# The first 55 microseconds of a two-part transformer kernel: x as the second load, vector copies on ScalarE, wide column products and more warming matmuls

## What is computed

```
c_act = silu(c)
mod = c_act @ w_ada[l] + b_ada[l]
sh_m, sc_m, gt_m, sh_f, sc_f, gt_f = split(mod, 6)
h = rms_norm(x, g_mix[l]) * (1 + sc_m) + sh_m
proj = h @ w_in[l]
qa, ka, va, qb, kb, vb, gate_logits = split(proj, ...)
```

## Time and profile before

| | us |
|---|---|
| runs of the kernel before | 1434.23, 1434.84, 1433.21 (median 1434.23) |
| the profiled execution's own time | 1432.99 |
| its span, first to last instruction | 1431.1 |
| TensorE busy (share of the span) | 1390.8 (97%) |
| VectorE busy | 924.7 (65%) |
| ScalarE busy | 757.9 (53%) |
| DMA, mean over the span | 192 GB/s |

### The profile page before, as it was taken

How to read it: one execution, slowest core, us unless ns; L and a number is a source line. 1 busy time by engine, 2 the same in 40 slices (tenths; PEclk the granted TensorE clock), 3 DMA queues, 4 the chain that set the end, 5 groups by cost and what they waited for, 6 DMA issues and landing times.

```text
span 1431.1 us, 19203 instructions
## 1 busy us (share of the span) xinstructions
PE 1390.8 (97%) x7039; PEld 1156.4 (81%) x7039; DVE 924.7 (65%) x1401; ACT 757.9 (53%) x1249; POOL 80.4 (6%) x133
## 2 busy tenths in 40 slices
PE   4999999999999999999899999999999999999998
PEld 4878877899988888887778888888888877788886
DVE  5677786798777554478986555476545556675453
ACT  4457746655456444366576444455444567574442
POOL 3011100000000000021300000000000100000000
PEclk9999999999999999999999999999999999999999
DMA  9897655477745755544355665547555463565540
GB/s 352 289 306 244 203 180 177 156 257 235 242 142 186 231 186 189 168 133 148 118 176 184 220 199 177 176 138 259 178 192 191 125 207 118 191 231 181 187 166 30
DMA packets 177596, 274.36 MB, mean 192 GB/s; under 512 B 6465, under 2 KB 120897, under 8 KB 177505
## 3 DMA queue, kind: packets, MB, share of 16 engines
q1 hardware_dynamic: 170800, 250.87, 52.9%
q0 software_dynamic: 5552, 20.20, 4.6%
q10 hardware_dynamic: 1153, 2.07, 0.5%
HBM read 272.05 MB, written 1.06 MB: 191 GB/s over the span
## 4 chain that ended last, share of the span: by engine, by line
PE 76%; DVE 5%; issue 1%; ACT 1%; DMA 0%; POOL 0%; DVEq 0%; POOLq 0%; SPq 0%; ACTq 0%
PE psum L2541 22%; PE psum L2543 22%; PE psum L2542 22%; PE psum L2581 2%; PE psum L2584 2%; PE psum L2583 2%; PE psum L2786 1%; DVE w_lo L2136 1%; PE psum L2638 1%; PE psum L2710 1%; PE psum L2739 0%; DVE PR L2476 0%; DVE attn L2313 0%; PE psum L2653 0%; DVE work L2290 0%
## 5 line engine op out<-in xcount | busy, mean ns | idle before, releaser
L2136 DVE TENSOR_TENSOR w_lo<-raw,w_hi 128x1024 fp32r<-128x1024 f32 (+1 forms) x312 | 371.8, 1234 | 114.4 <-ACT w_hi L1925 113.5
L1925 ACT ACTIVATE w_hi<-raw 128x1024 fp32r<-128x1024 f32 (+1 forms) x312 | 310.7, 1050 | 101.2 <-PE psum L2543 64.4
L2541 PE MATMUL psum<-w_hi,hT_hi 128*128 128x512 f32 x888 | 356.1, 401 | 6.9 <-DVE hT_lo L2236 3.7
L2543 PE MATMUL psum<-w_hi,hT_lo 128*128 128x512 f32 x888 | 347.2, 391 | 0.0
L2542 PE MATMUL psum<-w_lo,hT_hi 128*128 128x512 f32 x888 | 346.9, 391 | 0.0
L2541 PEld LDWEIGHTS psum<-w_hi,hT_hi 128*128 128x128 f32 x888 | 167.4, 189 | 46.2 <-issue 10.5
L2543 PEld LDWEIGHTS psum<-w_hi,hT_lo 128*128 128x128 f32 x888 | 167.2, 188 | 36.1
L2542 PEld LDWEIGHTS psum<-w_lo,hT_hi 128*128 128x128 f32 x888 | 167.6, 189 | 32.5 <-issue 0.5
L2136 DVE TENSOR_TENSOR lo_qk<-raw,hi_qk 128x1024 fp32r<-128x1024 f32 (+1 forms) x72 | 84.1, 1207 | 31.1 <-ACT hi_qk L1925 31.0
L2541 PE MATMUL psum<-w_hi,hc_hi 128*128 128x512 f32 x256 | 100.3, 392 | 0.6 <-DVE hc_lo L2461 0.6
L2543 PE MATMUL psum<-w_hi,hc_lo 128*128 128x512 f32 x256 | 99.8, 390 | 0.0
(11 more groups left out here) (236 smaller groups left out, 2334.8 us busy)
## 6 DMA issues: line engine op xcount, KB each, us to landing
raw<-in_ffn_wg_dram SPq DMA_DIRECT2D x88, 512.0 KB, 3.9
raw<-in_ffn_wu_dram SPq DMA_DIRECT2D x88, 512.0 KB, 5.0
raw<-in_ffn_wd_dram SPq DMA_DIRECT2D x44, 1024.0 KB, 4.9
raw<-in_w_up_dram SPq DMA_DIRECT2D x44, 512.0 KB, 4.9
raw<-in_w_in_dram SPq DMA_DIRECT2D x19, 1024.0 KB, 7.5
ada_raw<-in_w_ada_dram POOLq DMA_DIRECT2D x24, 512.0 KB, 5.3
raw<-in_even_w_in_dram SPq DMA_DIRECT2D x12, 1024.0 KB, 5.1
raw<-in_odd_w_in_dram SPq DMA_DIRECT2D x12, 1024.0 KB, 5.6
```

The costliest lines, as they stand in the source:

```text
L1925: nc.scalar.activation(hi_of(s)[:, cs], raw_of(s)[:, cs], ACT.Copy).then_inc(ready, 1)
L2136: nc.vector.tensor_tensor(lo_of(u)[:, cs], raw_of(u)[:, cs], hi_of(u)[:, cs].bitcast(F32), ALU.subtract)\
L2541: nc.tensor.matmul(o, a_hi, b_hi, start=start, stop=False)
L2543: return nc.tensor.matmul(o, a_lo, b_hi, start=False, stop=stop)
```

## The change

- x is loaded by SP, behind the first unit of `w_ada`, and no longer by GpSimd's queue.
- The four copies of the vectors are made by ScalarE, behind the squares; VectorE only waits for them in front of the statistic, which has moved up between the sums of the first two `w_ada` units.
- The column products have 128 equal moving columns (`c_act` broadcast, a square of ones) in place of one. Both kinds now add up in the same place, so that VectorE needs one addition for a block in place of two; it reads every 128th column.
- `warm` waits for nothing: eight matmuls directly behind the turn of `c`, ten behind the vectors' turns, six behind the column products of block 2.
- The modulated reads of a bank are split by k-tile: two steps of one k-tile each, so `hT_lo` is made in two instructions of 128 x 256.
- The last unit of each four early ones is loaded in two halves (`early_second`).
- The plan's order: the column sum of block 0 and its bias addition come before the last sums of block 2. The split of unit 1 comes behind the first modulated reads, that of unit 2 behind the second. In the second round the column sum of block 1 comes before all sums of block 3, and va's k-tiles are spread between.

```diff
@@ build_plan @@
     ada(0, 0)
+    vector_uses = [pl.use(b) for b in (4, 5, 6, 7)]
+    pl.add("warm", bank=7, times=8)
+    st = tile_stat()
+    squared = x_squares(st, (0, 1), [("x_loaded", 16)] * TT)
+    pl.add("vectors", uses=vector_uses)
+    var(st, (0, 1), squared, False, EPS)
     shared = shared_ada(0, 0, 3)
-    vector_uses = [pl.use(b) for b in (4, 5, 6, 7)]
-    pl.add("vectors", uses=vector_uses)
-    st = x_stats([("x_loaded", 16)] * TT)
-    pl.add("warm", use=vector_uses[3], times=8)
+    pl.add("normalise", st=st, half=0)
+    pl.add("warm", bank=1, times=10)
+    turned_rows = [turn_early(G, ("scr_ready", scr_version()), ("mod", 1), ("mod", 0), 0, 2),
+                   turn_early(G, None, ("mod", 1), ("mod", 0), 2, 3)]
     ada(2, 0)
-    pl.add("normalise", st=st, half=0)
-    rest = turn_early(G, ("scr_ready", scr_version()), ("mod", 1), ("mod", 0), 0, (2, 3))
+    adasum(0, shared=shared)
     shared2 = shared_ada(2, 1, 3)
...
     pl.split_to(0)
-    adasum(0, shared=shared)
+    adasum(2, shared=shared2)
+    pl.add("warm", bank=0, times=6)
+    pl.add("modfinal", vec=1, gain=0, half=0)
+    turned_rows[0]()
     pl.split_to(1)
-    adasum(2, shared=shared2)
-    pl.add("modfinal", vec=1, gain=0, half=0)
-    rest[0]()
+    turned_rows[1]()
     pl.split_to(2)
-    rest[1]()
...
     pl.split_to(3)
+    product_step("proj", va[1][0], ks=(0,), inc=None)
+    adasum(1, shared=shared)
     ada(3, 0)
-    product_step("proj", va[1][0], ks=(0,), inc=None)
+    product_step("proj", va[1][0], ks=(1,), inc=None)
+    turned_rows = [turn_early(G, ("scr_ready", v), ("mod", 1), ("mod", 0), 4, 2)]
     shared3 = shared_ada(3, 3, 3)
-    adasum(1, shared=shared)
+    product_step("proj", va[1][0], ks=(2,), inc=None)
     adasum(3, shared=shared3)
-    rest = turn_early(G, ("scr_ready", v), ("mod", 1), ("mod", 0), 4, (2, 3))
-    product_step("proj", va[1][0], ks=(1, 2, 3))
+    product_step("proj", va[1][0], ks=(3,))
+    turned_rows.append(turn_early(G, None, ("mod", 1), ("mod", 0), 6, 3))
     pl.add("modfinal", vec=1, gain=0, half=1)
...
@@ column products @@
-                                nc.tensor.matmul(psum[:, use.bank, 4 + j:5 + j],
+                                nc.tensor.matmul(psum[:, use.bank, j * P:(j + 1) * P],
                                                  w[:, k * BANK + j * P:k * BANK + (j + 1) * P],
-                                                 c_act[:, 4 + k:5 + k], start=k == a["own"][0], stop=k == 3)
+                                                 c_act[:, 4 + k:5 + k].to_broadcast([P, P]),
+                                                 start=j == 0 and k == a["own"][0], stop=False, skip_group_check=True)
...
-                            ins = nc.tensor.matmul(psum[:, use.bank, j:j + 1], acc[:, j * P:(j + 1) * P],
-                                                   ones[:, 0:1], start=True, stop=True)
+                            ins = nc.tensor.matmul(psum[:, use.bank, j * P:(j + 1) * P], acc[:, j * P:(j + 1) * P],
+                                                   ones[:, 0:P], start=a["unit"] is None and j == 0, stop=True,
+                                                   skip_group_check=True)
```

82 lines of the change are left out of this document (46 added, 36 removed).

## The result

The change takes 1437.46 us (median of ten runs, 1436.97 to 1439.80), the kernel before 1434.78 in the ten runs beside it (1433.21 to 1436.41). The ratio is 1.0021, with a 95% interval of 1.0013 to 1.0029: **+2.7 us**. The interval leaves out 1, so the change is slower, if by only about what a measurement here can tell. The forecast was 1436.0 in a range of 1431.4 to 1439.0, most likely "no change that can be told"; the measured time lies between it and the slower rival's 1437.9. The profiled execution took 1437.91, span 1436.1. That is 4.9 over the profiled execution of before, so the two profiles differ by 2.2 us more than the medians.

A forecast was written before the change was run, and what follows sets the result against it. TensorE, busy 97%, was taken as the bound, with VectorE leading after T. T = 25.5 plus 29.3 gave U = 54.8 against 53.05, +1.75 us: 1436.0 against the median 1434.23, range 1431.4 to 1439.0.

The forecast's parts named there:

- slower rival: Ahead of U: TensorE's 3.1 us without work drops the clock, +1.7 us, to 1437.9; chance 20%.
- T: Start of ACT's first modulated turn: forecast 25.5 against 26.12 before; 23.4 with the upper clock level, 26.0 with the lower.
- The statistic: Step behind x's squares and the vector copies, ahead of the normalised rows: forecast at 13.6, 2.7 us sooner.
- the wait for the first column product: VectorE waiting for TensorE before its column add, ahead of T: 0.1 to 2.6 us, taken as 2.1.
- the warm-up holds: At the start: warming matmuls run up to the turns, clock up, T 23.4, U 52.7, time 1433.9; chance 27%.
- the second set: ACT's modulated turns started by the second modulation vector: forecast at T + 25.1, before at T + 21.7.
- The sums of block 1: VectorE's next sums after the low halves of unit 2: forecast at T + 8.25, before at T + 6.3.
- the stall: VectorE standing before the last sums of the second round, behind the column add: a new 2.15 us.
- U: Start of the fifth weight unit's first product on TensorE: forecast T + 29.3 = 54.8 against 53.05, +1.75 us.
- the last wait for TensorE's columns: TensorE's four last column products before the second vector's add and hand-over: 1.0 us.
- The row: Trace evidence for column products: eight one-column passes take 1.03 us, held by weight loads, as 128 columns do.
- What follows moves by what U moves: After U the instruction list is the same, so the time moves by U's shift, forecast +1.75 us.

The follow-up runs named there:

- second profile: The change, unaltered, profiled once more in one execution beside one of the kernel before: 1440.59 us, the kernel before 1436.59.
- filled gap: The change with twelve more warming matmuls behind va's last k-tile, ahead of the last four turns: 1434.75 us, ratio 1.0002.
- early high half: The change with the high half of unit 1 made on ACT before the first modulated turns: 1436.23 us, ratio 1.0014.
- all together: The change with the second round's sums in a row, later first addition, earlier high halves and the fifth unit's low half split: 1430.14 us, ratio 0.9973.
- reordered variant: The change with its second round (column sums of blocks 1 and 3, va's k-tiles) in the order of before: 1435.34 us, ratio 1.0003.
- wide columns: The kernel before with only the column products of 128 equal columns and the single bias addition: 1432.85 us, ratio 0.9987.
- no warming: The change without its three groups of warming matmuls (24 in all): 1438.06 us, ratio 1.0028.
- late addition: The change with the first vector's column add behind the following unit's four sums and six warming matmuls in another bank: 1437.38 us, ratio 1.0020.
- narrow columns: The change with the single-column products and the two column adds of the kernel before: 1439.64 us, ratio 1.0035.

## Why the prediction was right, and what was off

The time lies in the range, and the path was the right one: what VectorE's list gives away behind T eats the early start. But the forecast's own narrower range, +0.9 to +2.5, was missed by 0.2, the moments on the path came out right in part through misses of opposite sign, and the clock, which the forecast held at 1.00, fell.

**The start.** The statistic was forecast for 13.6 and came at 13.58, and by luck: x landed at 10.43 for 9.9, so the squares ended at 12.83 for 12.3, and the four copies behind them, put at 1.2 us, took 0.61 (12.74 to 13.35). A third miss was hidden by the squares. The vectors' rows were to land at 8 and landed at 11.17, for 11.02 before; in the other profiles with x on SP's queue they landed between 10.31 and 11.14. A queue with a megabyte less beside them helped by 0.7 us at most, not by three. By the rule of the Trainium skill, "DMA: Bandwidth & Descriptors", section Queues, rings and completion order, that each DMA engine takes the queues in turn, I had looked for an earlier landing; this trace does not show it. The copies I had bounded by ones of 8 and 256 columns and taken a middle value, but copies overlap: the second starts at 12.88, when the first, of 0.24 us from 12.74, is still running. The Trainium skill, "ScalarE: Activation LUTs", section What ACT_TABLE_LOAD costs, gives an ACTIVATE with immediate operands 186 ns and 0.833 ns a column, with an overlap of 93 ns between neighbours; by it the four would take an estimated 0.74, nearer than my figure.

**T.** Forecast 25.5, measured 24.30 and 23.81. The term that was off is the wait for the first column product: 2.1 us forecast, 1.16 and 0.66 measured. It was priced with the lower clock through the turns and most of the column products. The rival "the warm-up holds" had the mechanism for this part: with the vectors' rows late, the warming matmuls ran until 16.7, and the clock was up at 17.7, or 15.0 in the second profile. Its T of 23.4 lies 0.4 to 0.9 below, since VectorE waits a little even then. Its end, 1433.9, did not come about, for what happened behind T.

**From T to the second set.** The sums of block 1 were forecast at T + 8.25 and came at T + 8.06; the stall 2.15, measured 2.44; the second set at T + 25.1, measured T + 25.7; U at T + 29.3, measured T + 30.0 in both profiles. The forecast's own terms for the second set add up to T + 24.95. Most of the rest is the last wait for TensorE's columns, put at 1.0 and measured at 1.73 (49.53 above). This part of the prediction stands, and the runs show its causes: the high half of unit 1 behind T costs 1.0 us, the order of the second round 3.1 us in the second set (T + 22.6 for T + 25.7). U came out at +1.26 (+0.78 in the second profile) for the forecast's +1.75, because the T that was 1.2 too late was partly made up by 0.7 too little behind it.

**The clock ahead of U.** The forecast held it at 1.00; the rival with 20% let it fall and priced it at 1.7 us. It fell in both profiles, for 1.7 and 2.7 us, and in three of the four variants that left the gap, which makes five of six. So the profiled time is the forecast's path, shorter by 0.5, with this rival's price on top. For the median the argument is the filled gap, which takes 2.7 us off. The chance was too small: I had counted against it that single columns had preceded both earlier falls. It fell here with 128 columns too, so they are not needed for it, but not always, as the variant with the early high half shows (3.48 us, no fall). The gap's length alone does not settle it: a gap of 3.13 us at 79, in the variant with all together, left the clock at 1.00, and one of 1.88 in the reordered variant did in one profile and not in the other. The gap with matmuls in it kept the clock twice of two.

**Wide columns.** The row had them cost nothing, against the rule of the Trainium skill, "TensorE: Matmul & The Clock Gate", section Back-to-back issue gap. Row and runs agree (1.03 and 1.05 us), the rule's 2 us do not show. What I missed is their gain: at U I allowed 1.7 us of cleaner products and said that none of it would reach it. Alone, in the kernel before, they brought U forward by 1.24, since there TensorE's own queue, with the second set's turns and the products behind them, sets U. In the changed kernel VectorE does, as I had said.

**Behind U.** "What follows moves by what U moves" was too strong. The wait for the next modulation rows added 0.6 in the first profile, and the load near 270 added 1.1. ScalarE's wait for that load is 3.45 to 3.98 us in six profiles (before, wide columns, filled gap twice, no warming, all together) and 4.48 to 4.91 in seven (change twice, order twice, early high half, late addition, narrow columns). In the three programs profiled twice both executions agree, so it goes with the program; its cause is open, and no variant was made for it. The 1.9 between 85 and 150 in the second profile of the change is open too.

## What to carry over

A start that is 2 us earlier is worth nothing if the leader behind it is another engine whose list also grew: follow the moment to where the bounding engine runs without a gap again. Adding an in-order wait on VectorE for TensorE's result costs all that stands behind it, so put the work that waits for nothing ahead of the addition. And price every gap of some microseconds on TensorE twice, once as idle time and once as the products behind it at half the clock, or fill it with matmuls that nobody reads.

## What was unexpected of the hardware

The clock can fall without a gap in front. In the kernel before TensorE has none over 0.15 us from 28.92 to 71, and the clock fell at 46.1, in the midst of 32 single-column records that start at 42.92; with wide ones it did not. In the narrow variant it fell at 20.2, with TensorE at work from 16.25 to 20.16; with wide ones in that place it did not in any of nine profiles. But this is no rule, as 32 single-column records of the narrow variant's second round went by at 1.00. The moment of the clock's rise differs between executions of the same program, 15.0 and 17.7, and moves T by 0.56 us. An earlier U can be eaten by the clock: it came 1.33 us earlier, and 1.0 of that was gone by 58, because the stretch at 0.50 then began at 51.6 and covered the unit's first twelve products. And of thirteen profiles four (no warming, and the three taken later) show one more stretch at 0.50 near 700, in the midst of work that has only gaps of about 1 us there, and the lag grows by 0.5 to 0.6 us.
